# Second attention: row sums inverted four heads at a time and spread by a matrix product, two kinds of work moved to GpSimd, row maxima taken two heads ahead

## The reference, cut to what matters

```python
s = jnp.einsum('bhqd,bhkd->bhqk', q_blk, k).astype(jnp.float32) * (FOX_HEAD_DIM ** -0.5)
s = s + (c_q[..., :, None] - c_k[..., None, :])      # c: running sum of log forget gates
s = jnp.where(pos_k[None, :] <= pos_q[:, None], s, -jnp.inf)
p = jax.nn.softmax(s, axis=-1)
return jnp.einsum('bhqk,bhkd->bhqd', p, v.astype(jnp.float32))
...
o = o * jax.nn.sigmoid(gate.astype(jnp.float32))
return (o.astype(h.dtype) @ w_out).astype(h.dtype)
```

## Time and profile before

| | |
|---|---|
| median of 3 runs | 1980.48 us (1980.27 to 1980.97) |
| the profiled execution | 1980.89 us |
| its span in the trace | 1979.1 us |
| busy: TensorE, VectorE, ScalarE, GpSimd | 1814.4, 922.0, 604.6, 90.4 us |
| granted TensorE clock, mean | 0.937 |
| attention stage | about 1374 to 1550 us of the span |

### The profile page before, as it was taken

How to read it: one execution, slowest core, us unless ns; L and a number is a source line. 1 busy time by engine, 2 the same in 40 slices (tenths; PEclk the granted TensorE clock), 3 DMA queues, 4 the chain that set the end, 5 groups by cost and what they waited for, 6 DMA issues and landing times.

```text
span 1979.1 us, 20578 instructions
## 1 busy us (share of the span) xinstructions
PE 1814.4 (92%) x8225; PEld 1431.3 (72%) x8225; DVE 922.0 (47%) x1272; ACT 604.6 (31%) x785; POOL 90.4 (5%) x122
## 2 busy tenths in 40 slices
PE   4899988989999889999999698998888989999997
PEld 1367754668888677888878577986766778888886
DVE  3556233565666545444433444322787543333233
ACT  1123111472222324333322253333343233232221
POOL 0000000001100000000000100000232100000000
PEclk8899999589999889999999799999898989999998
DMA  7233100015544423333233222125886233332231
GB/s 256 88 123 103 65 0 22 1 44 185 167 159 165 133 64 86 102 90 94 72 96 102 66 67 72 55 65 76 29 30 40 65 85 85 102 91 81 83 99 57
DMA packets 213285, 171.45 MB, mean 87 GB/s; under 512 B 5268, under 2 KB 202772, under 8 KB 213126
## 3 DMA queue, kind: packets, MB, share of 16 engines
q1 hardware_dynamic: 205190, 139.76, 29.5%
q0 software_dynamic: 8000, 30.38, 4.6%
HBM read 163.70 MB, written 2.10 MB: 84 GB/s over the span
## 4 chain that ended last, share of the span: by engine, by line
PE 81%; DVE 12%; ACT 3%; issue 2%; DMA 1%; DVEq 0%; SPq 0%; ACTq 0%; POOL 0%
PE PS L417 21%; PE PS L418 21%; PE PS L419 21%; PE PS L426 4%; DVE RS L110 2%; PE PS L885 2%; PE PS L544 1%; PE PS L1789 1%; DVE JUNK L119 1%; DMA WS<-in_w_mod 1%; PE PS L986 1%; DVE SQ L102 1%; DVE WL L91 1%; DVE X L102 1%; PE PS L445 1%
## 5 line engine op out<-in xcount | busy, mean ns | idle before, releaser
L417 PE MATMUL PS<-XH,WH 128*128 128x512 f32 (+1 forms) x1280 | 492.1, 384 | 6.3 <-DVE WL L91 4.7
L418 PE MATMUL PS<-XL,WH 128*128 128x512 f32 (+1 forms) x1280 | 493.1, 385 | 0.0
L419 PE MATMUL PS<-XH,WL 128*128 128x512 f32 (+1 forms) x1280 | 490.8, 383 | 0.0
L91 DVE TENSOR_TENSOR WL<-WS,WH 128x2048 fp32r<-128x2048 f32 (+1 forms) x129 | 272.7, 2114 | 264.8 <-ACT WH L87 263.9
L417 PEld LDWEIGHTS PS<-XH,WH 128*128 128x128 f32 x1280 | 241.8, 189 | 60.7 <-DVE WL L91 4.5
L418 PEld LDWEIGHTS PS<-XL,WH 128*128 128x128 f32 x1280 | 241.4, 189 | 49.4
L419 PEld LDWEIGHTS PS<-XH,WL 128*128 128x128 f32 x1280 | 241.9, 189 | 48.7
L87 ACT ACTIVATE WH<-WS 128x2048 fp32r<-128x2048 f32 (+1 forms) x129 | 228.6, 1772 | 78.5 <-PE PS L419 61.5
L417 PE MATMUL PS<-HH,WH 128*128 128x512 f32 x352 | 137.3, 390 | 2.1 <-DVE WL L91 2.1
L418 PE MATMUL PS<-HL,WH 128*128 128x512 f32 x352 | 137.1, 389 | 0.0
L419 PE MATMUL PS<-HH,WL 128*128 128x512 f32 x352 | 137.1, 389 | 0.0
(11 more groups left out here) (323 smaller groups left out, 2565.9 us busy)
## 6 DMA issues: line engine op xcount, KB each, us to landing
WS<-in_w_in SPq DMA_DIRECT2D x24, 1024.0 KB, 5.2
WS<-in_ffn_w_up SPq DMA_DIRECT2D x44, 512.0 KB, 4.9
WS<-in_ffn_w_in SPq DMA_DIRECT2D x44, 512.0 KB, 4.8
MSRC<-in_w_mod POOLq DMA_DIRECT2D x32, 512.0 KB, 4.6
WS<-in_fox_w_in SPq DMA_DIRECT2D x16, 1024.0 KB, 5.6
WS<-in_ffn_w_down SPq DMA_DIRECT2D x16, 704.0 KB, 4.6
WS<-in_ffn_w_out SPq DMA_DIRECT2D x16, 704.0 KB, 4.7
WS<-in_w_mod SPq DMA_DIRECT2D x8, 1024.0 KB, 11.2
```

Source lines behind the costliest of these rows:

```text
L91: self.e.tensor_tensor(o, a, b, op).then_inc(*self.done.to(*key))
L417: e.matmul(o, lh, rh, start=first and i == 0, stop=False)
L418: e.matmul(o, lh, rl, start=False, stop=False)
L419: ins = e.matmul(o, ll, rh, start=False, stop=last and i == n - 1)
```

## The change

**Row sums.** The 64-wide reciprocal for each head and GpSimd's product with the gate are gone. In their place:

- VectorE multiplies the head's unnormalised output by the gate, in place in FG (`fx_gated`).
- ScalarE copies one row of the sums to row 32 j of a tile SUMS, j being the head's place in its group (`fx_sum`).
- VectorE inverts the whole tile once for a group (`fx_inverse`). The groups are the heads 0 to 3, 4 to 7, 8 to 11, 12 and 13, 14 and 15.
- TensorE spreads two rows of it over the two halves of 128 partitions with one float32 product, 128x512 (`fx_spread_pe`, with the constant matrix E4). It goes into the values bank that `fx_gated` and `fx_sum` have just emptied.
- VectorE multiplies FG by the result for a whole pair at once, 128x512 (`fx_out`).

**GpSimd** gets the diagonals (SHIFT) and the rests of the queries (QO). **Row maxima** are taken two heads ahead: round h has the rows and maxima of head h + 2 where it had those of h + 1. The load of NCK keeps its two buffers and its wait for the maxima of head h - 2, now `fx_max_dve`.

The diff, cut to its core:

```diff
 def fx_split_dve(v, m):
-        v.e.wait_ge(*acts.at("fx_q_hi", m))
-        v.tt(QO[:, m, :], QT[:, m, :], QS[m % 2][:, :].bitcast(F32), ALU.subtract, key=("fx_lo", m))
+    def fx_split_pool(g, m):
+        g.e.wait_ge(*acts.at("fx_q_hi", m))
+        g.tt(QO[:, m, :], QT[:, m, :], QS[m % 2][:, :].bitcast(F32), ALU.subtract, key=("fx_q_lo", m))
...
 def fx_values_pe(e, h):
         if h >= 2:
-            e.wait_ge(*dve.at("fx_out", h - 2))
+            e.wait_ge(*dve.at("fx_gated", h - 2))
+            e.wait_ge(*acts.at("fx_sum", h - 2))
+        if h in SPREADS:
+            e.wait_ge(*dve.at("fx_out", SPREADS[h]))
...
+    GROUPS = [0, 4, 8, 12, 14, 16]
+    INVERSES = {5: 0, 9: 1, 13: 2, 15: 3, 16: 4}
+    SPREADS = {6: 0, 7: 1, 10: 2, 11: 3, 14: 4, 15: 5, 16: 6, 17: 7}
+    def fx_spread_pe(e, n):
+        m = SPREADS[n]
+        g, j = group(2 * m)
+        e.wait_ge(*dve.at("fx_inverse", g))
+        e.wait_ge(*dve.at("fx_gated", n - 2))
+        e.wait_ge(*acts.at("fx_sum", n - 2))
+        e.matmul(bank(6 + n % 2), E4[:, j // 2, :], SUMS[g % 2][:, :], start=True, stop=True).then_inc(
+            *pe.to("fx_spread", m))
     def fox_pe(e):
         fx_rows_pe(e, 0)
-        for h in range(17):
+        fx_rows_pe(e, 1)
+        for h in range(18):
             if h < 16:
                 fx_scores_pe(e, h)
-            if h + 1 < 16:
-                fx_rows_pe(e, h + 1)
-            if h:
+            if h + 2 < 16:
+                fx_rows_pe(e, h + 2)
+            if h in SPREADS:
+                fx_spread_pe(e, h)
+            if 1 <= h < 17:
                 fx_values_pe(e, h - 1)
...
     def fox_act(a):
+                a.act(SUMS[g % 2][32 * j:32 * j + 1, :], bank(6 + (h - 1) % 2, p0=r, p1=r + 1), ACT.Copy,
+                      key=("fx_sum", h - 1))
...
     def fox_dve(v):
         for h in range(18):
-            if h + 1 < 16:
-                fx_shift_dve(v, h + 1)
-            if 1 <= h < 17:
-                p0, p1, r0, r1 = halves(h - 1)
-                e.wait_ge(*pe.at("fx_values", h - 1))
-                v.rcp(RS[(h - 1) % 2][p0:p1, :], bank(6 + (h - 1) % 2, p0=r0, p1=r1), key=("fx_rcp", h - 1))
-            if 2 <= h < 18:
-                v.tt(TF[p0:p1, :], bank(6 + g % 2, p0=p0, p1=p1), RS[g % 2][p0:p1, :], ALU.mult, key=("fx_out", g))
+            if h + 2 < 16:
+                fx_max_dve(v, h + 2)
             if h % 2 and 2 <= (h + 3) // 2 < 8:
                 fx_split_dve(v, (h + 3) // 2)
+            if 1 <= h < 17:
+                e.wait_ge(*pe.at("fx_values", h - 1))
+                v.tt(gate, bank(6 + (h - 1) % 2, p0=a0, p1=a1), gate, ALU.mult, key=("fx_gated", h - 1))
+            if h in SPREADS:
+                e.wait_ge(*pe.at("fx_spread", m))
+                v.tt(TF[:, :], FG[m][:, :], bank(6 + h % 2), ALU.mult, key=("fx_out", m))
+            if h in INVERSES:
+                e.wait_ge(*acts.at("fx_sum", GROUPS[g + 1] - 1))
+                v.rcp(SUMS[g % 2][:, :], SUMS[g % 2][:, :], key=("fx_inverse", g))
...
     def fox_pool(g):
         for h in range(18):
+            if h % 2 and 2 <= (h + 3) // 2 < 8:
+                fx_split_pool(g, (h + 3) // 2)
+            if h + 2 < 16:
+                fx_shift_pool(g, h + 2)
```

More of the change, by code:

```diff
@@ L280, in build @@
     VP = [room(f"VP{i}", [128, 5, 128], F32, 20.625 + 2.5 * i) for i in range(2)]
-    RS = [room(f"RS{i}", [128, L], F32, 25.625 + 2 * i) for i in range(2)]
+    SUMS = [room(f"SUMS{i}", [128, L], F32, 25.625 + 2 * i) for i in range(2)]
+    E4 = zone("E4", [128, 2, 128], F32, 71)
     TF = room("TF", [128, L], F32, 29.625)
@@ L1836, in fx_shift_dve @@
             e.wait_ge(*pe.at("fx_rows", h, i // 2))
[L1837 to L1841, removed]
+            v.add_min(JUNK[:, 0:w], PS[:, o:o + w], NCK[h % 2][:, 0:w], BT[:, h % 2, i:i + 1], key=("fx_max", h))
     def fox_dve(v):
@@ L1872, in fx_value_pool, with fx_shift_pool @@
         g.cp(VP[x][0:16, 4, 64 * x:64 * x + 64], VF[0:16, 4, 64 * h:64 * h + 64], key=("fx_v", h))
+    def fx_shift_pool(g, h):
+        g.e.wait_ge(*dve.at("fx_max", h))
+        if h >= 2:
+            g.e.wait_ge(*pe.at("fx_scores", h - 2, 2))
+        g.tt(SHIFT[h % 2][:, :].rearrange("p (i q) -> p i q", i=4), ID[:, :].unsqueeze(1).broadcast_to([128, 4, 128]),
+             BT[:, h % 2, :].unsqueeze(2).broadcast_to([128, 4, 128]), ALU.mult, key=("fx_shift", h))
     def fox_pool(g):
@@ L1879, in fox_pool @@
                     g.memset(z[i][64 - 64 * x:128 - 64 * x, x, :].bitcast(F32), 0.0, key=("fx_zero",))
+        fx_split_pool(g, 0)
         e.wait_ge(*pe.at("fg", 7))
+        fx_shift_pool(g, 0)
         for x in range(2):
             g.memset(VP[x][:, :, 64 - 64 * x:128 - 64 * x], 1.0)
-        e.wait_ge(*acts.at("v", 19))
         fx_value_pool(g, 0)
+        fx_shift_pool(g, 1)
+        for i in range(2):
+            g.memset(SUMS[i][:, :], 1.0, key=("fx_sums_one",))
+        fx_split_pool(g, 1)
         fx_value_pool(g, 1)
         for h in range(18):
[L1887 to L1891, removed]
+            if h % 2 and 2 <= (h + 3) // 2 < 8:
+                fx_split_pool(g, (h + 3) // 2)
+            if h + 2 < 16:
+                fx_shift_pool(g, h + 2)
             if 1 <= h < 15:
                 fx_value_pool(g, h + 1)
-            if h >= 3 and h % 2:
-                m = (h - 3) // 2
+            if h in SPREADS:
+                m = SPREADS[h]
                 e.wait_ge(*acts.at("fx_o_hi", m))
@@ L2041, in gpsimd @@
         e.dma_start(E2[:, :, :], A["e2"]).then_inc(landing("e2"), 16)
+        e.dma_start(E4[:, :, :], A["e4"]).then_inc(landing("e4"), 16)
         fox_pool(g)
@@ L2120, in constants @@
             e2[2 * m + x, m, 64 * x:64 * x + 64] = 1.0
+    e4 = np.zeros((128, 2, 128))
+    for j in range(4):
+        e4[32 * j, j // 2, 64 * (j % 2):64 * (j % 2) + 64] = 1.0
     out = dict(dft=dft, dct4=dct4, four_l=four_l, four_c=four_c, feats=feats, decay=decay, inv_cnt=inv, band=band,
-               flip=flip, causal=causal, e16=e16, e2=e2, ident=np.eye(128))
+               flip=flip, causal=causal, e16=e16, e2=e2, e4=e4, ident=np.eye(128))
     return {k: np.ascontiguousarray(v, dtype=np.float32) for k, v in out.items()}
```

51 lines of the change are left out of this document (34 added, 17 removed).

## The result

The changed kernel takes 1991.43 us (median of 4 runs, 1987.21 to 1993.02) beside 1980.38 us for the kernel before on the same chip (4 runs, 1979.97 to 1980.97). The ratio is 1.0052, with a 95% interval of 1.0035 to 1.007: slower by 11.1 us. The forecast was 1994.0, within 1981 to 2001. The profiled execution took 1987.21 us, with a span of 1985.2.

The account below looks back on a forecast made before the run. VectorE (9.0 us a head) and the loads (9.3 to 9.4) were taken as two near-equal bounds, the loads staying. 1980.9 + 6.6 for the end's steps + 6.5 for the clock gave 1994.0 us, range 1981 to 2001.

Parts of the forecast that it names:

- The loads bind the new kernel: Attention stage body: loads stay back to back at about 9.43 us each; only 1.5 us of gaps is gained.
- the 9.2 to 9.5 that I named as a sign: Attention stage: sign of a right forecast, landings of NCK still 9.2 to 9.5 us apart.
- The loads bind the kernel before: Attention stage before the change: loads run almost without a pause, 9.3 to 9.4 us a head, maxima lagging up to 3.
- two bounds of nearly the same height: Attention stage before the change: VectorE at 9.0 and loads at 9.3 to 9.4 us a head; the change lowers one.
- Steps of the end: From load 15's landing to the output product: TensorE stalls for inverses, product 6.6 us later than before, without clock effects.
- VectorE's three: End of the stage: gating 0.8, output of a pair 0.8 and inverse 3.4, together 5.0 us, while TensorE idles.
- The clock: End of the stage: three TensorE restarts at a lower clock, 2.2 us each, 6.5 in sum (range 5.4 to 10.4).
- the 0.4 for hops: End of the stage: six hops between engines add 0.4 us together before the output product.
- GpSimd at nothing: Attention stage: diagonals and query rests moved to GpSimd, 8.3 of 18.8 us a pair, cost nothing while loads set the pace.
- The loads don't bind: Rival, chance 0.10: stage body runs at TensorE's 7.7 us a head, saving 22, less 13 at the end: 1972 us.
- The body starves: Rival, chance 0.17: TensorE waits up to 4.6 us for spreads mid-stage, loads then issue too late: 1999 to 2004 us.
- A short end: Rival, chance 0.09: clock stays high, inverse cheaper than 3.4 us, loads give another 3 us: 1981 to 1984.

Follow-up runs that it names:

- dram_after: Changed kernel with CT written once to HBM and the loads of NCK reading their rows from there: 1957.1 us, ratio 0.9884 to the kernel before.
- dram_before: Kernel before the change, with CT written once to HBM and the loads of NCK reading their rows from there: 1979.55 us, ratio 0.9997.
- clock_held: Changed kernel with float32 products that nobody reads ahead of the last three spreads, plus a wait for head 15's maxima: 1984.92 us, ratio 1.0027.
- one_after: Changed kernel with rows, maxima and diagonals one head ahead instead of two: 1987.4 us, ratio 1.0039 to the kernel before.
- one_end: Changed kernel with all inverses but the last ahead of the maxima, last spread inside the output product, rows, maxima and diagonals one head ahead: 1976.96 us.
- dram_moves: Changed kernel with row sums inverted head by head as before (diagonals, query rests and earlier maxima kept), NCK loaded from HBM: 1969.3 us, ratio 0.995.

## Why the prediction was right

**The loads bind the new kernel: right.** VectorE's 54.9 us of waiting and landings 130.5 us apart (forecast: 1385.7 to 1516.2, the same 130.5) say it, and dram_after proves it by taking them away. The mean distance of 9.3 us is the forecast's; single distances go from 6.0 to 10.2, and only one of fourteen lies within the 9.2 to 9.5 that I named as a sign. By the rule of the Trainium skill (SBUF — State Buffer, section on the DMA port swizzle) that a transfer within four neighbouring partitions reaches one port, of about 27 GB/s, taken for the source, the loads would take 9.9 us each, as an estimate from that page. Ten of the fourteen distances are 9.8 to 10.2, which agrees; the 7.8, 6.0 and 7.7 are shorter than the rule would have them, and the mean is 29 GB/s.

**The loads bind the kernel before: wrong as I meant it.** I read the loads as running "almost without a pause" there and the maxima as lagging behind, and called it two bounds of nearly the same height. That there are two is right. But the loads were not the one that held: dram_before takes them away and gains nothing. The sum didn't suffer, since it only needed the bound that stays, and because the two lie so close: 132.0 us between landings 1 and 15 before, 130.5 with the loads alone. That closeness was luck for this reading; the DMA share of 0.91 showed that little room was left, not which bound held.

**Steps of the end**, counted from the landing of load 15 (the forecast without the clock first, then measured): to the end of the first inverse 6.9 and 6.8; spread, values, scores, spread, values 10.65 and 13.2; VectorE's three 5.0 and 5.0; spread and values 3.7 and 5.75; VectorE's three 5.0 and 5.0; last spread 1.0 and 1.1. The order of events and VectorE's durations hold throughout.

**The clock: right in kind, and off by 1 us at most.** I took 2.2 us for each of three restarts, 6.5 in sum. What the stretches behind the stops take at the full clock is seen in clock_held: 10.5, 3.7 and 0.6 us, where the changed kernel took 13.2, 5.75 and 1.1. So the restarts cost 2.6, 2.1 and 0.5 us up to the output product, and behind it 0.3 (437.2 us of span remain, beside 436.8 in the kernel before) to 1.2 (beside 436.0 in clock_held). That is 5.5 to 6.4 us, and clock_held as a whole gave back 6.5 by the medians. The third restart was taken too high, the first too low. The other part of the miss is in the steps without the clock: from the landing of load 15 to the output product they come to 31.7 us (36.95 less 5.2) and not 32.7, mostly because the last spread holds the product back by 0.6 and not 1.0 and the 0.4 for hops doesn't show. With +10.9 us at the product and 0.3 behind it, 1980.9 becomes 1992.1, against 1994.0 forecast and 1991.4 measured. That the median is so close is in part chance: the beginning of the stage alone moves by up to 6 us between traces.

**GpSimd at nothing: right**, with room: a diagonal took 1.09 us and a query rest 1.35, not 1.54, and in the changed kernel nothing waited for a diagonal.

**The rivals.** *The loads don't bind* was the wrong case for this kernel, but dram_after is that case made true, and I had put its gain too low: 1972, when it measures 1957.1. Beside dram_before the body saves 32.9 us (133.5 to 100.6 between landings), not 22: the round of a head fell from 9.5 us to 7.2, where I had counted 9.43 to 7.7, and over 14 distances, not 13. The end cost 10 us more, not 13. *The body starves* did not come: spreads in the middle of the stage waited twice, 5.8 us together between 1380 and 1500 in the changed kernel, the longer 3.1 (by the terms of the forecast up to 4.7, which it gives as 4.6), and the landings stayed as close together as forecast. *A short end* did not come either; each of its three conditions failed.

**Not settled:** why the stage begins up to 6 us earlier in some executions; what makes the loads 7, 11 and 15 land closer to the ones ahead of them; whether another source within SBUF would do as well as HBM; and the reading of one_after and one_end above, which no run takes apart.

## What to carry to other kernels

Where two bounds have nearly the same height, work taken off one of them gives nothing, and it is an experiment on each, not the shares of busy time, that tells which one holds: here the edit of the loads alone gave 0, the change alone cost 11 us, and both together gave 23. Work grouped to save an engine (an inverse for four heads) moves to a place behind the last arrival; look at what stands between the last transfer and the next stage, and put there only what that transfer feeds. A pause of TensorE such as the ones of 4.5 to 5.1 us here costs what stands in the waits and then again in the products that follow it at the lower clock.

## What the runs showed of the hardware

- A load of NCK spreads one row of 2,112 bytes over 128 partitions, 270 KB in all. From one partition of SBUF it lands 12.1 us after its issue when alone, and in ten of fourteen cases 9.8 to 10.2 us behind the load ahead of it in a queue of them (6.0 to 9.4 in the others). From a row in HBM it lands 2.9 to 3.4 us after its issue (the last one 4.4 to 4.7). The write of CT to HBM and the wait for it didn't make the kernel before longer (1979.55 with them, 1980.06 without in the same runs).
- A reciprocal on VectorE takes 3.35 us for 512 elements a partition, on 64 partitions (from PSUM) and on 128 (from SBUF).
- Products that nobody reads, put in place of three pauses of 4.45 to 5.07 us, made the kernel 6.5 us faster by the medians: with them the granted clock was 1.00 from 1515 to 1555, without them 0.50 to 0.85 in six of eight windows of that stretch.
- GpSimd's subtraction KO, 128x512, took 1.54 us in the kernel before and 1.28 in the changed one, where VectorE is busy for 80 us of the stage and not 125. VectorE's share isn't what sets it: in dram_moves VectorE is busy for 124 us of 168, and KO is at 1.28 too. VectorE's KLZ went the other way, 0.875 to 1.07 us, and 1.29 in dram_moves. In the kernel before, the diagonals and query rests are VectorE's, in the other two GpSimd's; whether this is the cause wasn't tried.
